# Hybrid decoder trunk: running sums as rows read back from DRAM in the scan, one root for three tiles' norms, and five waits moved

## The reference

```
def step(state, inp):
    cum = cumsum(dtc * A, axis=1)                       # 128 steps a chunk, per head
    seg = cum[:, :, None] - cum[:, None]
    L = exp(where(tril, seg, -inf))
    xdt = xc * dtc[..., None]
    cb = einsum('btgn,bsgn->btsg', cc, bc)
    y_diag = einsum('btsgh,bsghp->btghp', cb[..., None] * L, xdt)
    y_off = einsum('btgn,bghpn->btghp', cc, state) * exp(cum)[..., None]
    decay = exp(cum[:, -1:] - cum)
    new_state = state * exp(cum[:, -1]) + einsum('bsgn,bsghp->bghpn', bc, xdt * decay[..., None])
```

## Time and profile before

| | |
|---|---|
| median of 3 runs | 1541.9 us (1541.83 to 1542.55) |
| profiled execution | 1541.77 us, span 1540.0 us |
| PE busy | 1495.2 us, 97% |
| DVE, ACT, POOL busy | 861.8, 577.8, 272.8 us |
| mean granted TensorE clock | 0.987 of full |

### The profile page before, as it was taken

How to read it: one execution, slowest core, us unless ns; L and a number is a source line. 1 busy time by engine, 2 the same in 40 slices (tenths; PEclk the granted TensorE clock), 3 DMA queues, 4 the chain that set the end, 5 groups by cost and what they waited for, 6 DMA issues and landing times.

```text
span 1540.0 us, 19953 instructions
## 1 busy us (share of the span) xinstructions
PE 1495.2 (97%) x7481; PEld 1213.5 (79%) x7481; DVE 861.8 (56%) x1123; ACT 577.8 (38%) x869; POOL 272.8 (18%) x294
## 2 busy tenths in 40 slices
PE   9979999998999999999999999998999999999999
PEld 7768888787788887888788777776787888887887
DVE  5657776854544444332687758899555444444222
ACT  6447666643323232222233353435324323232110
POOL 4433333102100000000000045766222000000000
PEclk9979999999999999999999999999999999999999
DMA  8200010212232323233232230011131222323232
GB/s 324 86 25 29 28 56 5 106 56 82 82 109 82 109 82 109 83 109 109 83 109 82 82 109 28 28 54 55 56 110 59 106 98 92 109 82 109 83 109 82
DMA packets 20890, 130.68 MB, mean 85 GB/s; under 512 B 2400, under 2 KB 3040, under 8 KB 6496
## 3 DMA queue, kind: packets, MB, share of 16 engines
q1 hardware_dynamic: 20688, 127.80, 23.5%
q10 hardware_dynamic: 144, 2.10, 0.3%
HBM read 127.79 MB, written 2.10 MB: 84 GB/s over the span
## 4 chain that ended last, share of the span: by engine, by line
PE 79%; POOL 8%; issue 6%; DVE 4%; ACT 2%; POOLq 0%; DVEq 0%; ACTq 0%
PE ps L440 22%; PE ps L442 21%; PE ps L441 21%; PE ps L765 4%; POOL Lx L2082 3%; PE ps L745 2%; PE ps L725 2%; POOL sqacc L1989 1%; POOL xdd L2077 1%; PE ps L669 1%; PE ps L670 1%; POOL xdt L2074 1%; DVE wl L1425 1%; PE ps L741 1%; ACT wh L1032 1%
## 5 line engine op out<-in xcount | busy, mean ns | idle before, releaser
L1425 DVE TENSOR_TENSOR wl<-wraw,wh 128x2048 fp32r<-128x2048 f32 x111 | 257.8, 2323 | 251.2 <-ACT wh L1032 251.0
L440 PE MATMUL ps<-xh,wh 128*128 128x512 f32 (+2 forms) x912 | 359.0, 394 | 5.8 <-DVE xl L1435 3.4
L442 PE MATMUL ps<-xh,wl 128*128 128x512 f32 (+2 forms) x912 | 355.6, 390 | 0.0
L441 PE MATMUL ps<-xl,wh 128*128 128x512 f32 (+2 forms) x912 | 355.5, 390 | 0.0
L1032 ACT ACTIVATE wh<-wraw 128x2048 fp32r<-128x2048 f32 x111 | 211.7, 1907 | 185.7 <-PE ps L442 179.4
L440 PEld LDWEIGHTS ps<-xh,wh 128*128 128x128 f32 (+2 forms) x912 | 170.5, 187 | 43.7 <-issue 4.5
L442 PEld LDWEIGHTS ps<-xh,wl 128*128 128x128 f32 (+2 forms) x912 | 170.5, 187 | 37.5
L441 PEld LDWEIGHTS ps<-xl,wh 128*128 128x128 f32 (+2 forms) x912 | 170.6, 187 | 36.5 <-issue 0.7
L440 PE MATMUL ps<-hh,wh 128*128 128x512 f32 x352 | 138.6, 394 | 4.1 <-DVE hid L1510 4.1
L441 PE MATMUL ps<-hl,wh 128*128 128x512 f32 x352 | 138.1, 392 | 0.0
L442 PE MATMUL ps<-hh,wl 128*128 128x512 f32 x352 | 138.1, 392 | 0.0
(11 more groups left out here) (280 smaller groups left out, 2436.1 us busy)
## 6 DMA issues: line engine op xcount, KB each, us to landing
wraw<-wstream SPq DMA_DIRECT2D x111, 1024.0 KB, 4.7
cw<-cw_in SPq DMA_DIRECT2D x1, 4096.0 KB, 14.2
xT<-xT_in SPq DMA_DIRECT2D x8, 256.0 KB, 6.3
part<-xT_in ACTq DMA_DIRECT2D x1, 2048.0 KB, 9.0
out<-xT SPq DMA_DIRECT2D x8, 256.0 KB, 6.6
wraw<-wstream SPq DMA_DIRECT2D x4, 256.0 KB, 5.7
wraw<-wstream SPq DMA_DIRECT2D x2, 512.0 KB, 7.5
rows<-rows_in SPq DMA_DIRECT2D x1, 276.0 KB, 7.7
```

What stands on the lines that cost most here:

```text
L440: mm(o, wa[0], xa[0], start=start, stop=False)
L441: mm(o, wa[0], xa[1], start=False, stop=False)
L442: return mm(o, wa[1], xa[0], start=False, stop=stop)
L1425: TTo(wl[:, s, :], wraw[:, s, :], wh[:, s, :].bitcast(F32), ALU.subtract).then_inc(lo_done, 1)
```

## The change

- **Scan.** `Gm` and its 32 matmuls are gone. PE's sums of `dtb` (bank 6) are copied to `cum`, turned once by PE, copied to `cumT` and stored to DRAM. For each chunk a DMA on ACT's queue reads eight rows back into all partitions (`rowc`, 512 KB); ACT forms `seg` with eight Relu of 128 x 128 (input scale -1, bias a column of `cum`) and exponentiates `seg` instead of PSUM. Loads are issued two chunks ahead.
- **z tiles** alternate between banks 0 and 5 and wait for the tile before the last. The first z products use banks 0, 1, 3, 5. In group step 0 the first third of z stands ahead of `to_features`.
- `split_lo(n0 + 4)` stands behind y in step 3. `dt_f` is copied ahead of two `to_tokens`. In the last group `yh` and `yl` of the first eight tiles come ahead of the decays and y, and the output halves rotate through banks 5, 0, 1.
- **Norms.** Tile 0 keeps its own root; tiles 1 to 3 share one of 128 x 18. `split_lo(6)` stands behind three `transposed_lo`.
- **Waits.** `residual`, `ffn` and the SSD input projection no longer wait for the last evacuation. FFN's first gate uses banks 4 and 5; column sums and broadcast stand in its third chunk; the down projection waits for the gates' reads (`gate_in`) instead of the last `hid`. The squares behind the SSD output move into the FFN. `o_rest` of the last group stands ahead of the last `add_part`.

```diff
+FIRST_Z_BANKS = (0, 1, 3, 5)
...
         def half_bank(t):
-            return 6 if t == 6 else 5
+            return (5, 0, 1)[t % 3]
+        def z_bank_of(tt):
+            return 5 if tt % 2 else 0
...
-        LATE = {1: EVAC["nsa_out"]}
+        LATE = {1: EVAC["nsa_out"], 3: EVAC["ssm_out"]}
...
             def residual(name, x, ready=None, late=None):
-                pe.wait_ge(evac, t0)
...
             def ffn(up, down, L):
-                pe.wait_ge(evac, t0)
...
+                chunk_F(n0, None, 0, xs, range(KT), (4, 5), True, True, each=fresh(L))
+                chunk_F(n0 + 1, None, 0, xs, range(KT), (2, 3), True, True, before=first_up)
+                chunk_F(n0 + 2, None, 0, xs, range(KT), (0, 1), True, True, inside=sums)
+                chunk_F(n0 + 3, None, 0, xs, range(KT), (2, 3), True, True, before=lambda m: pe.wait_ge(evac, t0 + 1 + m))
...
+                pe.wait_ge(gate_in, hidden)
                 pe.wait_ge(hl_done, hidden - 4)
...
-            def decays(g, j):
-                for q in range(2):
-                    pe.wait_ge(g_built, g * 8 + (2 * j + q + 1))
-                    after(pe, seg_exp, g * 8 + (2 * j + q - 1))
-                    mm(ps[:, q, :], tri[:, 1, :], Gm[:, q, :, :].rearrange("p h t -> p (h t)"), start=True, stop=True
-                       ).then_inc(seg_mm, 1)
+            def chunk_products(g, j):
...
-                        pe.wait_ge(evac, g * 4 + (t0 + 4 + tt))
+                        pe.wait_ge(evac, g * 4 + (t0 + 4 + tt - 1))
...
-                places = {0: ((), (), (0, 1, 2)), 1: ((0,), (1,), (2,)), 2: ((0,), (1,), (2,)), 3: ((0, 1), (2,), ())}
+                places = {0: ((), (0,), (1, 2)), 1: ((0,), (1,), (2,)), 2: ((0,), (1,), (2,)), 3: ((0, 1), (2,), ())}
...
+                if tt == 1:
+                    pe.wait_ge(cum_copied, 1)
+                    pe.transpose(ps[:, 7, 0:P], cum[:, :], ident[:, :]).then_inc(cumT_mm, 1)
...
+            act.wait_ge(cumT_done, 1)
+            act.dma_start(cum_rows, cumT[:, :]).then_inc(rows_stored, 16)
...
             def decays(g, j):
+                act.wait_ge(row_landed[j % 2], g * 32 + 16 * (j // 2 + 1))
                 for q in range(2):
-                    act.wait_ge(seg_mm, g * 8 + (2 * j + q + 1))
+                    after(act, seg_exp, g * 8 + (2 * j + q - 1))
+                    for h in range(4):
+                        ins = A(seg[:, q, h, :], rowc[:, j % 2, 4 * q + h, :], ACT.Relu, scale=-1.0,
+                                bias=cum[:, bass.ds(at_ + 4 * q + h, 1)])
+                    ins.then_inc(seg_built, 1)
+                for q in range(2):
+                    act.wait_ge(seg_built, g * 8 + (2 * j + q + 1))
                     after(act, y_mm, g * 8 + 2 * (j - 1))
-                    A(Lx[:, j % 2, q, :, :], ps[:, q, :].rearrange("p (h t) -> p h t", h=4), ACT.Exp
-                      ).then_inc(seg_exp, 1)
+                    A(Lx[:, j % 2, q, :, :], seg[:, q, :, :], ACT.Exp, scale=-1.0).then_inc(seg_exp, 1)
+                if not isinstance(g, int) or 4 * g + j + 2 < 4 * SG:
+                    row_load(g, j + 2)
...
             def qk_norm(tt, g):
-                rstd(sm[:, 3, 0:6], sm[:, 1, 0:6], qk_mean, g * 4 + (tt + 1), qk_rstd)
+                if g == 0:
+                    if tt in (0, 1):
+                        t = slice(0, 1) if tt == 0 else slice(1, TT)
+                        pool.wait_ge(qk_mean, t.stop)
+                        TTo(sm0[:, 2, t, :].rearrange("p t h -> p (t h)"), sm0[:, 1, t, :].rearrange("p t h -> p (t h)"),
+                            mhalf[:, 0:6 * (t.stop - t.start)], ALU.pow).then_inc(qk_rstd, t.stop - t.start)
```

More of the change, by code:

```diff
@@ L254, in trunk @@
         btst = a.take("btst", [P, 2, P])
-        Gm = a.take("Gm", [P, 2, 4, P])
+        seg = a.take("seg", [P, 2, 4, P])
+        rowc = a.take("rowc", [P, 2, SHP, P])
+        cum = a.take("cum", [P, P])
+        cumT = a.take("cumT", [P, P])
         Lx = a.take("Lx", [P, 2, 2, 4, P])
@@ L468, in chunk_F, with chunk_T @@
                         between(m)
-            def chunk_T(n, i, per, ks, width, first, last, before=None, each=None, bank=0):
+            def chunk_T(n, i, per, ks, width, first, last, before=None, each=None, banks=(0, 1, 2, 3)):
                 pe.wait_ge(lo_done, at(n + 1, i, per))
@@ L1087, in turn @@
                 def turn(i):
-                    split_hi(n0 + 1, i, 2)
-                    if isinstance(i, int) and L in LATE:
+                    if not isinstance(i, int) or i != 1:
+                        split_hi(n0 + 1, i, 2)
+                    if isinstance(i, int) and i == 0:
                         for t in range(KT):
@@ L1354, in group @@
                         split_hi(n0 + 3, g, 2)
+                    if last and k == 0:
+                        stage(g, 2)
+                        act.wait_ge(products, 2 * CHUNK["ssm_out"])
+                        act.wait_ge(yT_done, 2 * TT)
+                        for kt in range(0, FIRST_KT, 2):
+                            A(yh[:, :, kt:kt + 2, :], yT[:, :, kt:kt + 2, :], ACT.Copy).then_inc(yh_done, 1)
                     if last and k >= 2:
@@ L1401, in _ @@
             split_hi(n0 + 1)
-            for c in range(4):
-                if c < 3:
-                    split_hi(n0 + 2 + c)
-                for m in range(2):
-                    square(2 * c + m, NORM["ssm_out"], None, 0, t0)
+            for c in range(3):
+                split_hi(n0 + 2 + c)
+            act.wait_ge(products, 2 * (n0 + 4))
             for kt in range(KT):
+                act.wait_ge(evac, t0 + kt + 1)
                 x_hi(NORM["ssm_out"], kt)
@@ L1729, in _ @@
             transposed_lo(0, (0, 1, 2), lambda h: h)
+            split_lo(6)
             dve.wait_ge(kc_sq, 1)
@@ L1897, in group @@
                         split_lo(n0 + 3, g, 2)
-                    if k < 2 or not last:
-                        build_g(g, k + 2)
-                    if k == 3 and not last:
-                        split_lo(n0 + 4, g, 2)
+                    if last and k == 0:
+                        for kt in range(0, FIRST_KT, 2):
+                            y_lo(kt // 2 + 1, 2 * TT, slice(0, TT), slice(kt, kt + 2))
                     y = ybuf[:, k % 2, :]
@@ L1922, in group @@
                     TTo(y, y, zs[:, k, :], ALU.mult).then_inc(y_done, 1)
+                    if k == 3 and not last:
+                        split_lo(n0 + 4, g, 2)
                     if k or not first:
                         to_features(g, k - 1)
-                    if last and k == 0:
-                        for kt in range(0, FIRST_KT, 2):
-                            y_lo(kt // 2 + 1, 2 * TT, slice(0, TT), slice(kt, kt + 2))
                     if last and k == 1:
```

163 lines of the change are left out of this document (91 added, 72 removed).

## The result

The changed kernel takes 1498.3 us (median of 4 runs, 1497.4 to 1499.3) against 1542.0 us before: a ratio of 0.972, 95% interval 0.971 to 0.974. The forecast was 1496 us, the range 1486 to 1511. The profiled execution took 1497.7 us, 1.8 more than its span.

The account below looks back on a forecast made before the run. PE, busy 1495.2 of 1540.0 us, was taken to bound the kernel. Terms 18.9 + 2.9 + 6.0 + 2.7 + 5.1 + 7.5 + 3.2 = 46.3 us off 1541.8 gave 1496 us, range 1486 to 1511 (8 in 10).

Parts of the forecast that it names:

- The middle of the scan: Scan, 11 middle chunks: removed Gm matmuls and z waits, less new waits for a split, gain 18.9 us.
- Start of the scan: First chunks of the scan: gain 2.9 us, bounds -1 and +4, limited by the chain through two DMAs.
- There PE takes the thirteenth z matmul: Start of the scan: PE takes this matmul when split_lo(n0 + 3) ends, at 918.3, against 921.2 before.
- the rival of a bound ACT: Scan: ACT or DVE becomes the pace, middle gives 8 instead of 18.9, start loses 2; 1511 us, chance 0.15.
- Last group: Last group of the scan: 13.0 us off, new waits leave 7.7, a clock stretch takes 1.7; gain 6.0 us.
- Norms: Attention norms: shared root saves 0.75 us, moved split gives 2.0; gain 2.7 us, bounds 1 and 4.
- FFN ends: Ends of the two FFNs: waits of 4.1 us removed and twice 1.7 of clock; gain 7.5 us.
- Entry of the second FFN: Entry of the second FFN: 1.5 us of wait gained and 1.7 of clock; gain 3.2 us.
- the small waits: Outside the scan: PE's waits for xol 1.4, xT 1.5, sqacc 1.3 and xT of L1468 0.9 go; gain 5.1 us.
- The slower rival: Scan's row loads last over about 26 us because all partitions read the same 4 KB; slower than before, chance 0.03.
- The rival without new waits: Scan: the 1.4 us waits, the last group's 2.0 and 2.2 and clock stretch fall away; 1488 us, chance 0.13.
- That the small waits come back: FFN ends and entries: PE runs into the next late piece, clock stretches stay; 1505 us, chance 0.12.

Follow-up runs that it names:

- the six more Relus: Changed kernel with six more Relus of 120 columns a chunk on ACT, written to a scratch tile nobody reads: 1499.8 us, ratio 0.973.
- the two runs: Changed kernel with the split of weight chunk 6 back beside the norms: 1495.5 us; changed kernel with a root for every tile, split left moved: 1497.0 us.
- the earlier products: Changed kernel with chunk 0's products inside the last z tile and DVE's split of z+2 ahead of the staging of chunk 0: 1494.3 us, ratio 0.969.

## Why the prediction was right, and where it was off

- **The middle of the scan** (18.9 foretold, 18.6 between landmarks) is right in its mechanism and its size: PE is the pace, the z waits go, and two waits of 1.4 us for a split appear, which DVE's order causes; the run that changed this order took them away. That the `Gm` matmuls are won in full and the z waits go with the second bank follows from the sum and the wait list; no run tried these two alone.
- **Start of the scan** (2.9 foretold, 0.6 found): this is the term that was mis-sized. The chain through the two DMAs, Relu, `zs` and the splits ended within 0.3 us of the prediction, because errors cancelled, which is luck: the row came 1.4 us sooner, eight Relus took 0.75 us longer and the split beside POOL 0.66. For the Relu the trace before had a nearer row than the two that the prediction used (L1204, shown with the six more Relus). The step that failed is "There PE takes the thirteenth z matmul": PE had a wait of 1.8 us for POOL's `Lx` ahead of it, the clock fell behind it, and PE itself became late by 2.7 us. Filling the wait gave 3.0 us back. The prediction named this wait among its signs but gave it no price, and its sum left out POOL's two multiplies, which set when it ends: they took 4.47 us beside DVE's split, and 2.49 where the split had been moved.
- **ACT's load**: 28.0 us a group against 26.8 foretold; the rival of a bound ACT is out, since 27 us more of ACT cost 3.5, and DVE is busy for 30.1 us of a group's 39.4.
- **Last group** (6.0 and 6.1): the sum is right, by luck as far as the runs show, since two terms in it are not. The second wait for the scaled y was 1.1 us instead of 2.2. The stretch was charged with 1.7 us, but filling the wait won nothing, so it costs nothing beside DVE's `y_lo`. Those four pieces took 8.5 us beside POOL where the prediction left them as they were; that this is what took the place of the two was not tried.
- **Norms** (2.7 and 2.5): right sum, wrong split between the edits, as the two runs show.
- **FFN ends** (7.5; 7.9 by putting the wait back): right, the clock's share too. **Entry of the second FFN and the small waits** came out within 1 us of their terms.
- **The slower rival** is out: the row load lands in 3.6 us (median of the trace's issues) against the 26 from which it would have decided. (Its 1570 us for a load of 30 us is a slip: 15 chunks of 15 us instead of 9.7 add 80 us to the forecast, which gives 1575.) The rival without new waits is out as well: all of them are there, one at half its size. That the small waits come back is out: none of the named ones is in the list.

## What to carry to other kernels

Price a wait of the bounding engine together with the clock behind it, and ask first whether that engine is the pace in the stretch that follows: here the same low stretch cost 3 us at the start of the scan and nothing in the last group. Where a wait can't be removed, a few idle matmuls into a free bank are a cheap test of what the clock takes, and here they were worth keeping. When two edits remove one collision, undo each alone before giving either of them the gain.

## What the runs showed of the hardware that was not expected

The low stretch at 303 us, behind waits of 0.6 and 1.3 us, stands in seven of the thirteen traces behind this section, whose code at that place is the same, and is missing in the others; it moves a run by 1.6 to 1.7 us, and may be part of the spread of 1 to 4 us within a kernel's runs; with one trace for each kernel this is not shown. The low clock at the norms changes too: 13.7 us in the change's trace, 6.8 in that of the filled wait at the scan, 17.1 in that of the earlier products, and the edits of those two do not touch the norms. Ten matmuls of 128 x 512 in the wait ahead of the first y (1.8 us in PE's row) kept the clock at its upper level, and so did 18 in one of 4.4 us and 8 in one of 1.8, even with a wait of 3.0 us between the two. A DVE split of 128 x 2048 beside POOL nearly doubled two POOL multiplies of 128 x 512 (4.47 against 2.49 us) and did nothing to a POOL power of 18 columns (3.22 us with it and without).
